# Mixture of 16 experts in one layer: weights fetched in 4 KB pieces, low parts on VectorE alone, experts interleaved over their groups, and half of the result rows fetched during the last experts

## The reference, cut to what matters

```python
g_sel = jnp.argmax(lg, axis=-1)
...
le = jnp.take_along_axis(le, g_sel[:, None, None], axis=1)[:, 0]
p_e = jax.nn.softmax(le, axis=-1)
top_v, top_i = lax.top_k(p_e, TOP_K)
gates = p_sel[:, None] * top_v / jnp.sum(top_v, axis=-1, keepdims=True)
expert_ids = g_sel[:, None] * EXPERTS_PER_GROUP + top_i
...
hg = jnp.einsum('nd,edf->nef', xf, w_gate)
hu = jnp.einsum('nd,edf->nef', xf, w_up)
a = jax.nn.silu(hg) * hu * combine[:, :, None]
y = jnp.einsum('nef,efd->nd', a, w_down)
```

## Time and profile before

| | us |
|---|---|
| median of 3 runs (lowest, highest) | 510.84 (509.73, 511.15) |
| the profiled execution | 510.6 |
| its span, first to last instruction | 509.0 |
| PE busy | 439.7 (86%) |
| VectorE busy | 285.5 (56%) |
| ScalarE busy | 256.4 (50%) |
| GpSimd busy | 181.6 (36%) |

### The profile page before, as it was taken

How to read it: one execution, slowest core, us unless ns; L and a number is a source line. 1 busy time by engine, 2 the same in 40 slices (tenths; PEclk the granted TensorE clock), 3 DMA queues, 4 the chain that set the end, 5 groups by cost and what they waited for, 6 DMA issues and landing times. The chain is left out here.

```text
span 509.0 us, 7334 instructions
## 1 busy us (share of the span) xinstructions
PE 439.7 (86%) x2599; PEld 328.6 (65%) x2599; DVE 285.5 (56%) x434; ACT 256.4 (50%) x366; POOL 181.6 (36%) x186
## 2 busy tenths in 40 slices
PE   5999999999698999999999953899999999998200
PEld 4877877787586666667788742577666666665100
DVE  3535542355633645552230256489899999977136
ACT  4664333563434636462135642578777777765100
POOL 0383000514300000000123833456776776745070
PEclk9999999999989999999999965899999999999755
DMA  8872222223214000001595289899999999995276
GB/s 256 219 239 95 89 84 82 84 84 102 78 73 169 3 1 1 1 0 42 194 361 177 107 300 319 249 293 338 328 297 312 332 330 337 344 342 193 68 263 263
DMA packets 64486, 94.80 MB, mean 186 GB/s; under 512 B 11632, under 2 KB 44400, under 8 KB 64448
## 3 DMA queue, kind: packets, MB, share of 16 engines
q1 hardware_dynamic: 55376, 69.87, 43.0%
q0 software_dynamic: 5088, 17.89, 11.2%
q10 hardware_dynamic: 3984, 6.56, 3.6%
HBM read 81.27 MB, written 13.04 MB: 185 GB/s over the span
## 5 line engine op out<-in xcount | busy, mean ns | idle before, releaser
L1350 DVE TENSOR_TENSOR wlo<-raw,whi 128x2048 fp32r<-128x2048 f32 (+1 forms) x47 | 103.7, 2207 | 20.1 <-ACT whi L943 20.0
L1475 PE MATMUL bank<-whi,xT_hi 128*128 128x512 f32 x224 | 93.1, 416 | 3.1 <-DVE wlo L1041 2.2
L943 ACT ACTIVATE whi<-raw 128x2048 fp32r<-128x2048 f32 x45 | 86.2, 1915 | 10.5 <-PE bank L1477 5.5
L1477 PE MATMUL bank<-whi,xT_lo 128*128 128x512 f32 x224 | 88.8, 397 | 0.0
L1476 PE MATMUL bank<-wlo,xT_hi 128*128 128x512 f32 x224 | 88.6, 395 | 0.0
L646 POOL TENSOR_TENSOR wlo<-raw,whi 128x1024 fp32r<-128x1024 f32 x16 | 59.1, 3692 | 38.2 <-ACT whi L943 38.2
L1475 PE MATMUL bank<-whi,xsT_hi 128*96 128x512 f32 x128 | 52.5, 411 | 2.7 <-DVE xsT_lo L1356 2.7
L1476 PE MATMUL bank<-wlo,xsT_hi 128*96 128x512 f32 x128 | 51.4, 401 | 0.0
L1475 PEld LDWEIGHTS bank<-whi,xT_hi 128*128 128x128 f32 x224 | 42.7, 191 | 13.4 <-issue 4.1
L1477 PE MATMUL bank<-whi,xsT_lo 128*96 128x512 f32 x128 | 51.1, 399 | 0.0
L1477 PEld LDWEIGHTS bank<-whi,xT_lo 128*128 128x128 f32 x224 | 42.7, 191 | 9.7
(11 more groups left out here) (212 smaller groups left out, 766.8 us busy)
## 6 DMA issues: line engine op xcount, KB each, us to landing
raw<-in_w_gate_dram SPq DMA_DIRECT2D x32, 512.0 KB, 6.6
raw<-in_w_up_dram SPq DMA_DIRECT2D x32, 512.0 KB, 8.2
raw<-in_w_down_dram SPq DMA_DIRECT2D x32, 512.0 KB, 6.7
raw<-in_w_in_dram SPq DMA_DIRECT2D x9, 1024.0 KB, 5.1
expert_rows<-yout POOLq DMA_DIRECT2D x16, 384.0 KB, 5.7
raw<-in_w_out_dram SPq DMA_DIRECT2D x4, 1024.0 KB, 5.9
x_sb<-in_x_prompt_dram SPq DMA_DIRECT2D x8, 256.0 KB, 5.9
normed_tokens<-xn ACTq DMA_DIRECT2D x4, 512.0 KB, 3.9
```

The lines of the kernel that those rows point to most:

```text
L943: act.activation(whi[SPLIT_OF[m3]][:, :], eraw[slot][:, :], ACT.Copy).then_inc(m_hi, 1)
L1350: dve.tensor_tensor(wlo[SPLIT_OF[m3]][:, 0:n], eraw[slot][:, 0:n], whi[SPLIT_OF[m3]][:, 0:n].bitcast(F32), ALU.subtract).then_inc(m_lo, 1)
L1475: pe.matmul(acc, x_hi, w_hi, start=start, stop=False)
L1477: return pe.matmul(acc, x_lo, w_hi, start=False, stop=stop)
```

## The change

Four things.

- **Pieces.** `load_gate_up` reads input row 8p + c of an expert's `w_gate` or `w_up` into partition p (before: row 128k + p). A partition gets 4 consecutive rows of 256 values, 4 KB in one piece; before, four pieces of 1 KB. Gate and up then stand side by side in a unit as 1024 columns each, and a matmul reads its 512 columns as two runs of 256. The tokens must be turned in the same order, so each of the eight transposes reads every eighth value of `xs`.
- **Low parts.** GpSimd makes none in the expert loop; VectorE makes all 2048 columns of every unit. `m_lo_pool` is gone.
- **Order of experts.** Position n runs expert 4·(n mod 4) + n div 4: the first of each group, then the second of each, and so on. Rows of `expert_rows` go by position. In the first step ScalarE and VectorE take the tokens of expert 1 before the unit after next, in place of behind it.
- **Fetch.** The two rows of a token are sorted by position. The one that was run first stands in positions 0 to 11, since a group's fourth expert cannot be it. GpSimd fetches these five tiles' rows during the last experts (three after the store of position 11, two after that of 12), once the first 12 positions' rows are stored and the ring buffers 0 to 4 are used up. The other five gathers come right after the last store has landed, before the flag is read. VectorE adds all first rows, then all second rows.

```diff
             def load_gate_up(e, half, slot):
-                dst = eraw[slot][:, :].rearrange("p (k n) -> p k n", k=UK)
                 for j, w in enumerate((w_gate, w_up)):
-                    src = w[0, e, half * UK * P:(half + 1) * UK * P, :].rearrange("(k p) f -> p k f", p=P)
-                    sp_.dma_start(dst[:, :, j * FF:(j + 1) * FF], src).then_inc(m_ld[slot], 16)
+                    src = w[0, e, :, :].rearrange("(p c) f -> p (c f)", c=KC)[:, half * UK * FF:(half + 1) * UK * FF]
+                    sp_.dma_start(eraw[slot][:, j * UK * FF:(j + 1) * UK * FF], src).then_inc(m_ld[slot], 16)
...
+            def fetch_sooner(t):
+                pool.wait_ge(m_hi, 3 * (E - NG) + t + 1)
+                pool.wait_ge(m_lo, 3 * (E - NG) + t + 1)
+                fetch(0, t)
...
-                    if not (isinstance(i, int) and i == 0):
-                        lo(i, j, a)
...
-                for i in range(E - 1 - BODY, E):
+                for i in range(E - 1 - BODY, E - 2):
                     step(i, 0, 0, i % 2)
-                lo(E, 0, 0)
+                if first:
+                    pool.wait_ge(places_ok, 1)
+                    for p in range(2):
+                        pool.wait_ge(y_st[p], 16 * (E - NG) // 2)
+                    for t in range(3):
+                        fetch_sooner(t)
+                store(E - 4, 0)
+                if first:
+                    for t in range(3, NT):
+                        fetch_sooner(t)
+                store(E - 3, 1)
                 store(E - 2, 0)
                 store(E - 1, 1)
                 for p in range(2):
                     pool.wait_ge(y_st[p], 16 * (E // 2) * (r + 1))
...
             moe_gathers(0)
+            for t in range(NT):
+                fetch(1, t)
             pool.wait_ge(flag_ok, 1)
...
+            def choices_by_place():
+                later, sooner = r1[0], r1[1]
+                low, high = rk
+                dve.tensor_tensor(later[:, :], place[0][:, :], place[1][:, :], ALU.is_gt)
+                dve.tensor_tensor(sooner[:, :], place[0][:, :], place[1][:, :], ALU.is_le)
+                dve.tensor_tensor(low[:, :], place[0][:, :], place[1][:, :], ALU.min)
+                link(dve.tensor_tensor(high[:, :], place[0][:, :], place[1][:, :], ALU.max))
...
-                    if first:
-                        dve.wait_ge(m_lo, u0 + 3)
-                        lo(0, unit_at(i, 4, j, a)[0], u0 + 3)
                     if not last:
                         tokens_lo(i + 1, 1 - p)
+                    if first:
+                        lo(0, unit_at(i, 4, j, a)[0], u0 + 3)
                     times_up(i, p)
...
-                                              xs[p][:, (4 * b + k) * P:(4 * b + k + 1) * P], ident[0:CAP, 0:CAP])
+                                              xs[p][:, :].rearrange("s (q c) -> s c q", c=KC)[:, 4 * b + k, :], ident[0:CAP, 0:CAP])
...
-                    pe.wait_ge(m_lo_pool, (E + 1) * r + i + 2)
```

More of the change, by code:

```diff
@@ L116, in trunk_step @@
         pos_y = [sb(f"pos_y{i}", [P, NT], I32) for i in range(2)]
+        early_y = [sb(f"early_y{i}", [P, NT], I32) for i in range(2)]
         cnt = sb("cnt", [P, 1])
@@ L697, in _ @@
                     moe_gathers(r)
-                fetch(ROUNDS * SLOTS)
-            with pool.Else():
-                fetch(SLOTS)
+                for t in range(NT):
+                    for c in range(2):
+                        fetch(c, t, pos_y, (ROUNDS * SLOTS, ROUNDS * SLOTS))
             pool.wait_ge(st_out, 16)
@@ L1331, in _ @@
             link(ins)
+            place = rd
             for c in range(2):
-                ins = dve.tensor_scalar(pos_y[c][:, :], rk[c][:, :], float(SLOTS), None, ALU.add)
-            ins.then_inc(places_ok, 1)
+                ins = dve.tensor_scalar(place[c][:, :], rk[c][:, :], float(SLOTS), None, ALU.add)
+            link(ins)
+            def choices_by_place():
[5 more added lines that the diff above has]
+                link(dve.tensor_tensor(high[:, :], place[0][:, :], place[1][:, :], ALU.max))
+                own = r1[2], place[0]
+                swapped = r1[3], place[1]
+                for c, (pos, n) in enumerate(((low, FIRSTS), (high, SLOTS))):
+                    same, other = (sooner, later) if c == 0 else (later, sooner)
+                    dve.tensor_copy(pos_y[c][:, :], pos[:, :])
+                    ins = dve.tensor_scalar(early_y[c][:, :], pos[:, :], float(n - 1), None, ALU.min)
+                    dve.tensor_tensor(own[c][:, :], gate[0][:, :], same[:, :], ALU.mult)
+                    last = dve.tensor_tensor(swapped[c][:, :], gate[1][:, :], other[:, :], ALU.mult)
+                ins.then_inc(places_ok, 1)
+                link(last)
+                for c in range(2):
+                    ins = dve.tensor_tensor(gate[c][:, :], own[c][:, :], swapped[c][:, :], ALU.add)
+                link(ins)
             dve.wait_ge(r_exp, 1)
@@ L1420, in moe, with add_rows @@
                 out_rows(E - 1, 1, E // 2 - 1)
+            def add_rows(n):
+                for c, ld in enumerate((yg_first, yg_second)):
+                    for t in range(NT):
+                        p = rows[t]
+                        dve.wait_ge(ld[t], 16 * n)
+                        if c:
+                            dve.wait_ge(first_added, t + 1)
+                        dve.scalar_tensor_tensor(out=x_sb[0:p, t, :], in0=yg[c][t][0:p, :], scalar=gate[c][0:p, t:t + 1],
+                                                 in1=x_sb[0:p, t, :], op0=ALU.mult, op1=ALU.add).then_inc(y_ok if c else first_added, 1)
             moe(0)
@@ L1426, in _ @@
                     moe(r)
[L1429 to L1437 removed]
+                add_rows(2)
+            with dve.Else():
+                add_rows(1)
         @block.tensor
```

134 lines of the change are left out of this document (54 added, 80 removed).

## The result

| | before | after |
|---|---|---|
| median (lowest, highest), us | 511.0 (509.7, 511.5) | 503.47 (502.07, 508.06) |
| the profiled execution, its span | 510.6, 509.0 | 503.52, 501.6 |
| first token transposes to start of last matmul | 161.1 | 163.3 |
| start of last matmul to end of span | 34.4 | 24.4 |

The ratio of after to before is 0.9863 [0.9822, 0.9904]. The end gave 10.0 us, and TensorE's stretch, which was to get 4.7 us shorter, got 2.2 us longer.

A forecast was written before the change was run, and what follows sets the result against it. It took PE's own pace as the bound, loads slightly slower, then 33 us without PE work. Span 509.0 - 2.0 - 1.0 - 1.7 - 13.0 = 491.3 us, execution 493.1 us, range 487 to 506.5.

The forecast's parts named there:

- a sign of being wrong: PE from first token to last matmul, 161 us: if this gets longer, the forecast is wrong.
- The low parts: Expert steps: without GpSimd's half, PE gets back 0.15 us a step, 2.0 us over 13 steps (0 to 2.5).
- The transposes: Eight strided weight loads a step on PE: taken as free; upper bound 0.83 us a step, 12.5 us.
- The first step: PE's 1.50 us wait for expert 1's low parts shrinks by the turned order: 1.0 us (0 to 1.5).
- The table of places: About 2.3 us more VectorE work ahead of its first unit, hidden by a 3.7 us wait.
- The pieces: Weight loads: 4 KB pieces near 385 GB/s leave room for early fetches and end PE's last waits, 1.7 us (0 to 1.7).
- rival 3: Weight loads: no faster with 4 KB pieces, early fetches run ahead of the last units; about 500 us, chance 0.09.
- The end: After the last matmul: five late gathers in place of ten, issued before the flag is read; 13.0 us (11 to 14).
- Rival 2: Expert steps: VectorE becomes the bound if its 3.40 us stay; +6.9 us, 500.0 us, chance 0.09.

The follow-up runs named there:

- e5: The kernel before with three units of weights in flight in place of two; 511.59 us, ratio 1.0007.
- e3: The changed kernel with the 1 KB pieces and contiguous token transposes of before; median 508.4 us.
- e12: The changed kernel with the five result stores issued only after the last addition; 508.34 us, ratio 0.9945.
- e4: The changed kernel with three units of weights in flight in place of two; 496.09 us, ratio 0.9677.
- e7: The changed kernel with three units in flight, early fetches after the last two units landed, 1 KB pieces and contiguous transposes; 494.18 us, ratio 0.9665.
- e2: The changed kernel with the five early fetches issued only when the last two units of weights have landed; 499.5 us, ratio 0.9782.
- e9: The changed kernel with three in flight, fetches after the loads, normed tokens stored in turned order, one unit held until the first gather landed; 489.13 us.

## Why the prediction was wrong, point by point

PE's stretch got longer, which the prediction had named as a sign of being wrong. The steps took 2.3 us off it, the first steps 2.5, and 7.0 us came back at its end, where 1.7 were to be won.

- **The low parts** (0.15 us a step, 2.0 us): the mechanism was right, the size was not. They were worth 0.42 us a step. I had taken the wait as 389.59 less the end of the transposes at 389.40, and that end is modelled, so starts are better for reckoning. By starts it is 1.02 us against 0.60 with nothing to wait for. The same part also made the 1.07 us of the earlier trace rows, which I had put down to the loads (e5).
- **The transposes** (0, bounds 0 and 0.83 us a step): 0.21 us. Neither end was right: a load goes from 141 to 208 ns, half more, not double. The rule that I cited, the Trainium skill, "Advanced Engine Details and Errata", section "SBUF Cachelines", says that a new line with each value costs something; the traces agree, 208 ns against 141. The reason for zero, that a load has time for each value, fell. The two errors nearly cancelled: the step went down by 0.175 us, 2.3 us in all, against 2.0 in the sum.
- **The first step** (1.0 us, 0 to 1.5): right, at its upper bound. Expert 1's low parts come at 321.31 us, PE does not wait, and the whole 1.50 us are won. A further 1.0 us was luck: from the first to the second set of transposes PE took 6.27 us against 7.26 before, at a granted clock of 0.60 against 0.50, having reached the upper level sooner. e3 and e12 have 7.27 and 7.28 us there.
- **The table of places** (hidden): right. The first tokens' low parts start at 315.35 after 2.23 us idle.
- **The pieces** (1.7 us, and room for the fetches): this step failed. The 385 GB/s of the earlier trace rows were not the pace of 4 KB pieces: with 4 KB pieces everywhere and two units in flight the loads ran at 305 to 344. The limit of two in flight set the pace (e4), and the pieces were worth up to 4% (e7). A shorter step and 2.2 MB more then made PE wait 6.9 us for weights in its last steps, and the lower clock behind the longest wait cost some 1.5 us. The waits to be won from the loads were smaller too: of the 1.7 us, 1.07 were GpSimd's low part (e5). So TensorE's last matmul came at 477.2 in place of 469.9. That is rival 3: 500 us by its sum, 503.5 measured; I gave it 0.09.
- **The end** (13.0 us, 11 to 14): right in mechanism, 3.0 us short: 10.0. The first late gather came 7.7 us after the last matmul, not 5.9, as the last store took 5.25 us to land. The rows then came 1.9 us apart and not 1.27, the pace of their issue: 13.7 us from the first gather's issue to the last addition's end, not 12.5. The flag and the branch on VectorE cost 0.87 us, not 4.2, which was hidden.
- **Rival 2** (VectorE bound): did not come. The 3.40 us became 2.29; VectorE is busy for 19.03 of 20 us, and PE waits for nothing from 324 to 440 us.

## What to carry to other kernels

When an engine waits for loads and the DMA share reads 1.0, try a higher number of transfers in flight before their layout is changed: it is one number. It gains nothing where no engine waits for the loads (e5), and here it made the first gather 1.0 to 1.5 us later. When a step gets shorter, count anew whether the loads can keep its pace. While they cannot, put transfers that are needed later behind the last ones that are needed now (e2). Bulk loads beside a small urgent gather delay it by microseconds; a wait on the bulk queue won them back (e9).

## What the runs showed of the hardware

- The DMA rate was 305 to 344 GB/s with two units of 1 MB in flight (after) and 353 to 366 with three (e4), at shares of 0.98 to 1.01 and 1.02 to 1.03.
- TensorE's load of 128 float32 columns 32 bytes apart took 208 ns, contiguous 141; GpSimd's multiplication of 128x512 values took 1.29 us with a contiguous and with a strided output.
- GpSimd's issue of an indirect gather, 0.94 us, took 2.06 and 3.24 us beside VectorE's additions.
- After an idle time of 2.26 us TensorE's granted clock was 0.50, the lower level, for some 3 us, with matmuls of 512 columns starting 0.43 us apart in place of 0.23.
- The first gather of 0.39 MB took 8.7, 6.1 and 4.8 us to land, as fewer loads were started ahead of it.
